# First block of a two-block mixer on one core: gate columns of branches 0 and 2 placed ahead of their branches' paths

## The reference, cut to what matters

```python
h = _rmsnorm(x, mix_norm[l])
proj = (h @ w_in[l])                       # 2820 branch columns, then 3 * 1024 gate columns
ret_c, fox_c, rwkv_c, gate_c = split(proj)
y_ret  = retention branch(ret_c)           # 256 wide
y_fox  = forgetting attention(fox_c)       # 256 wide
y_rwkv = recurrent branch(rwkv_c)          # 256 wide
gates = sigmoid(gate_c)                    # (512, 3, 1024)
merged = gates[:, 0] * (y_ret @ p_ret[l]) + gates[:, 1] * (y_fox @ p_fox[l]) + gates[:, 2] * (y_rwkv @ p_rwkv[l])
x = x + merged @ w_out[l]
... feed-forward on the normed x
```

## Time and profile before

| what | value |
|---|---|
| runs | 3406.28, 3402.62, 3405.69 us |
| span of the profiled execution | 3410.4 us |
| TensorE busy | 3157.1 us (93%) |
| TensorE weight load busy | 2477.1 us (73%) |
| VectorE busy | 1743.8 us (51%) |
| ScalarE busy | 1298.9 us (38%) |

### The profile page before, as it was taken

One profiled execution on the slowest core, in us unless ns is written; L12 is line 12 of the kernel. 1 busy time (PEld: TensorE's weight loads), 2 busy tenths in 40 slices (PEclk: granted clock), 3 DMA queues, 4 the chain that ended last, 5 costly groups with the idle time before them and its releaser, 6 DMA issues.

```text
span 3410.4 us, 37439 instructions
## 1 busy us (share of the span) xinstructions
PE 3157.1 (93%) x14958; PEld 2477.1 (73%) x14958; DVE 1743.8 (51%) x2453; ACT 1298.9 (38%) x2009; POOL 14.9 (0%) x22
## 2 busy tenths in 40 slices
PE   6998999999999988999999999998679799979997
PEld 5566777788886656867888887776368587867886
DVE  4345434555433454425555334446665444548995
ACT  3133323433231332323333224445343533346883
POOL 0000000000000000000000000000000000000000
PEclk9898989999999989979999999999889899999998
DMA  4111102222332111002222321111100001248991
GB/s 154 43 34 50 38 22 68 93 99 96 95 102 82 44 34 53 26 32 93 97 95 98 117 98 63 56 62 37 37 32 32 31 26 56 100 180 312 388 360 56
DMA packets 77629, 306.13 MB, mean 90 GB/s; under 512 B 8208, under 2 KB 13072, under 8 KB 65680
## 3 DMA queue, kind: packets, MB, share of 16 engines
q1 hardware_dynamic: 69056, 284.88, 23.5%
q10 hardware_dynamic: 5808, 9.41, 0.8%
q0 software_dynamic: 2592, 9.44, 0.8%
HBM read 295.83 MB, written 7.86 MB: 89 GB/s over the span
## 4 chain that ended last, share of the span: by engine, by line
PE 82%; DVE 8%; ACT 5%; issue 4%; DMA 1%; ACTq 0%; POOL 0%; POOLq 0%; DVEq 0%
PE bank L371 19%; PE bank L372 18%; PE bank L373 18%; PE bank L366 2%; PE bank L368 2%; PE bank L367 2%; ACT flow_head L390 2%; DVE flow_rest L401 1%; PE bank L1140 1%; PE bank L2363 1%; PE bank L1831 1%; PE bank L1153 1%; PE bank L1913 1%; PE bank L2376 1%; PE bank L1047 1%
## 5 line engine op out<-in xcount | busy, mean ns | idle before, releaser
L371 PE MATMUL bank<-h_head,flow_head 128*128 128x512 f32 x2144 | 913.7, 426 | 26.9 <-DVE flow_rest L401 24.6
L401 DVE TENSOR_TENSOR flow_rest<-flow_raw,flow_head 128x1024 fp32r<-128x1024 f32 (+2 forms) x372 | 438.6, 1179 | 976.8 <-ACT flow_head L390 976.7
L372 PE MATMUL bank<-h_rest,flow_head 128*128 128x512 f32 x2144 | 853.5, 398 | 0.0
L373 PE MATMUL bank<-h_head,flow_rest 128*128 128x512 f32 x2144 | 853.1, 398 | 0.0
L390 ACT ACTIVATE flow_head<-flow_raw 128x1024 fp32r<-128x1024 f32 (+2 forms) x372 | 379.3, 1020 | 704.0 <-PE bank L373 701.5
L371 PEld LDWEIGHTS bank<-h_head,flow_head 128*128 128x128 f32 x2144 | 413.9, 193 | 154.9 <-issue 70.4
L372 PEld LDWEIGHTS bank<-h_rest,flow_head 128*128 128x128 f32 x2144 | 414.1, 193 | 89.7 <-issue 16.6
L373 PEld LDWEIGHTS bank<-h_head,flow_rest 128*128 128x128 f32 x2144 | 412.8, 193 | 91.0
L371 PE MATMUL bank<-ff_head,flow_head 128*128 128x512 f32 x352 | 136.9, 389 | 0.0
L372 PE MATMUL bank<-ff_rest,flow_head 128*128 128x512 f32 x352 | 136.9, 389 | 0.0
L373 PE MATMUL bank<-ff_head,flow_rest 128*128 128x512 f32 x352 | 136.9, 389 | 0.0
(11 more groups left out here) (601 smaller groups left out, 4805.7 us busy)
## 6 DMA issues: line engine op xcount, KB each, us to landing
flow_raw<-in_w_in SPq DMA_DIRECT2D x176, 512.0 KB, 3.2
ring<-in_experts SPq DMA_DIRECT2D x84, 1024.0 KB, 7.2
flow_raw<-in_w_gate_up SPq DMA_DIRECT2D x88, 512.0 KB, 3.2
flow_raw<-in_w_down SPq DMA_DIRECT2D x32, 512.0 KB, 3.4
flow_raw<-in_w_out SPq DMA_DIRECT2D x24, 512.0 KB, 3.2
flow_raw<-in_paths SPq DMA_DIRECT2D x24, 256.0 KB, 2.6
flow_raw<-in_w_down SPq DMA_DIRECT2D x16, 384.0 KB, 3.0
flow_raw<-in_path_b SPq DMA_DIRECT2D x8, 512.0 KB, 3.2
```

The costliest lines, as they stand in the source:

```text
L371: nc.tensor.matmul(ps[u.bank][:, :], wh[:, c:c + P], head, start=start, stop=False)
L372: nc.tensor.matmul(ps[u.bank][:, :], wh[:, c:c + P], rest, start=False, stop=False)
L373: last = nc.tensor.matmul(ps[u.bank][:, :], wr[:, c:c + P], head, start=False, stop=stop)
L401: nc.vector.tensor_tensor(self.parts_of[p.slot][1][:, 0:p.words], p.raw, f32(self.parts_of[p.slot][0][:, 0:p.words]), ALU.subtract).then_i ...
```

## The change

In a layer the order becomes: 22 projection units; 8 gate units of branch 0 (ticks 176 to 240); 8 path units of branch 0 (240 to 256); branch 1 as before (256 to 336); 8 gate units of branch 2 (336 to 400); 8 path units of branch 2 (400 to 416). Banks 6 and 7 serve all of these. Gates of branch 0 stay in `acc`, those of branch 2 in two new places and `sgf`; one of the new places lies over `lora`, so the second layer loads its part of `lora` again behind `table_a`, and retention waits for both. The stretches become: retention ticks 66 to 130, attention 130 to 242, recurrent branch 242 to 400 (the end that paces it is now that of branch 2's gate units).

```diff
-        pe.wait_ge(*k.table_a.at(16 * (l + 1)))
+        pe.wait_ge(*k.table_a.at(16 + 32 * l))
...
+    k.gate_early, k.gate_late = at("gate_early", 67, (4, S)), at("gate_late", 18, (2, S))
...
+            a.dma_start(k.lora[:, l, :], dram["lora_1"][:, l, :]).then_inc(*k.table_a.up(16))
...
-    k.times[l] = [flow.units[k.units_of[l][c]].end for c in (FOX_UNIT - 1, RWKV_UNIT - 1, GATE_UNIT - 1)]
+    for i in range(DC):
+        last = gate_unit(k, l, 0, i, dram)
+    k.times[l] = [flow.units[m].end for m in (k.units_of[l][FOX_UNIT + 7], last)]
+    k.times[l].insert(0, flow.units[k.units_of[l][FOX_UNIT - 1]].end)
+
+def gate_of(k, b, i):
+    if b == 0:
+        return k.acc[:, i, :]
+    if b == 1:
+        return k.sgf[:, i % 2, :]
+    return k.gate_early[:, i, :] if i < 4 else k.gate_late[:, i - 4, :] if i < 6 else k.sgf[:, i - 6, :]
+
+def gate_unit(k, l, b, i, dram):
+    nc, flow = k.nc, k.flow
+    piece, dst = flow.piece(dram["w_in"][l, GATE_UNIT + b * DC + i]), gate_of(k, b, i)
+    def scale(v, m):
+        return nc.vector.tensor_tensor(dst, k.ps[flow.units[m].bank][:, :], k.root[:, :], ALU.mult)
+    def squash(a, m):
+        k.tables(EXP_TANH)
+        a.wait_ge(*flow.emptied_by(m))
+        nc.scalar.activation(dst, dst, ACT.Tanh, scale=0.5).then_inc(*k.squashed.up())
+    return flow.unit(6 + i % 2, [(piece, c * P) for c in range(DC)], normed(k, 2 * l)(False), [(1, scale)], [(2, squash)])
+
 def branch_units(k, l, b, dram):
+    if b == 2:
+        for i in range(DC):
+            k.gates_end = gate_unit(k, l, b, i, dram)
     for i0 in range(0, DC, 2):
-        pieces = [flow.piece(dram["w_in"][l, GATE_UNIT + b * DC + i]) for i in (i0, i0 + 1)]
+        if b == 1:
+            gate_unit(k, l, b, i0, dram)
+            gate_unit(k, l, b, i0 + 1, dram)
         both = flow.piece(dram["paths"][l, b, i0 // 2])
-        gates = []
-        for q in range(2):
-            ...  (scale and squash into sgf)
-            gates.append(flow.unit((6 if b < 2 else 4) + q, ...))
...
-        end = flow.units[paths_end[l][1]].end
+        end = flow.units[paths_end[l][3]].end
```

More of the change, by code:

```diff
@@ L579, in vector_part @@
         flow.dve(rot(0))
-        v.wait_ge(*k.table_a.at(16 * (l + 1)))
+        v.wait_ge(*k.table_a.at(16 + 32 * l))
         for j in range(4):
@@ L1449, in mixer_units @@
         k.units_of[l][0:FOX_UNIT], k.units_of[l][FOX_UNIT:RWKV_UNIT], k.units_of[l][RWKV_UNIT:GATE_UNIT])
-    k.times[l] = [flow.units[k.units_of[l][c]].end for c in (FOX_UNIT - 1, RWKV_UNIT - 1, GATE_UNIT - 1)]
+    for i in range(DC):
[18 more added lines that the diff above has]
+    return flow.unit(6 + i % 2, [(piece, c * P) for c in range(DC)], normed(k, 2 * l)(False), [(1, scale)], [(2, squash)])
 def branch_units(k, l, b, dram):
     nc, flow, v, a = k.nc, k.flow, k.v, k.a
-    operand = normed(k, 2 * l)
+    if b == 2:
+        for i in range(DC):
+            k.gates_end = gate_unit(k, l, b, i, dram)
     for i0 in range(0, DC, 2):
-        pieces = [flow.piece(dram["w_in"][l, GATE_UNIT + b * DC + i]) for i in (i0, i0 + 1)]
+        if b == 1:
+            gate_unit(k, l, b, i0, dram)
+            gate_unit(k, l, b, i0 + 1, dram)
         both = flow.piece(dram["paths"][l, b, i0 // 2])
-        gates = []
-        for q in range(2):
[L1463 to L1472, removed]
         for q in range(2):
@@ L1481, in gated @@
                 v.wait_ge(*k.squashed.at((l * 3 + b) * DC + i + 1))
-                dst = k.acc[:, i, :] if b == 0 else k.sgf[:, q, :]
-                return nc.vector.scalar_tensor_tensor(dst, k.sgf[:, q, :], 1.0, k.ps[flow.units[m].bank][:, :], ALU.add, ALU.mult)
+                gate = gate_of(k, b, i)
+                return nc.vector.scalar_tensor_tensor(gate, gate, 1.0, k.ps[flow.units[m].bank][:, :], ALU.add, ALU.mult)
             def add(v, m, q=q, i=i):
                 v.wait_ge(*flow.emptied_by(m))
-                nc.vector.tensor_tensor(k.acc[:, i, :], k.acc[:, i, :], k.sgf[:, q, :], ALU.add).then_inc(*k.added.up())
+                nc.vector.tensor_tensor(k.acc[:, i, :], k.acc[:, i, :], gate_of(k, b, i), ALU.add).then_inc(*k.added.up())
             def heads(a, m, i=i):
@@ L2640, in third_memory @@
     k.ple = [at(f"ple_{n}", c, (4, S)) for n, c in enumerate((56, 60))]
-    k.router_landed, k.stored = k.loaded.over(80), [k.table_a.over(32), k.table_2.over(64)]
+    k.router_landed, k.stored = k.loaded.over(80), [k.table_a.over(48), k.table_2.over(64)]
     k.picked_landed = [Mark(sems, f"picked_landed_{n}") for n in range(2)]
@@ L3244, in stream @@
         mixer_units(k, l, dram)
-        paths_end.append([branch_units(k, l, b, dram) for b in range(3)])
+        paths_end.append([branch_units(k, l, b, dram) for b in range(3)] + [k.gates_end])
         def merged(first, l=l):
```

## The result

The changed kernel takes 3429.7 us (median of 5 runs, 3421.5 to 3442.0) against 3405.7 us of the kernel before, measured beside it: ratio 1.0069, 95% interval 1.0049 to 1.0088. A second comparison gave 1.0054 (1.0039 to 1.0069). It is slower, as the forecast's likeliest case said, but by 18 to 24 us where 7 were forecast. That is outside the forecast's own 3409 to 3421 us and nearest to rival C (3434).

The account below looks back on a forecast made before the run. TensorE bounds the kernel, 82% of the chain that ended last. Per layer 14.0 us won and 17.5 us lost make 3.5 us slower, 7 in all: 3413 us, own range 3409 to 3421, overall range 3384 to 3436.

Parts of the forecast that it names:

- rival C: Costs in full: inputs lose 13 us, end 10, only 9 won; 14 us per layer slower, 3434 us; chance 0.14.
- The end of the branch (+7.5): Behind the recurrent branch's result, VectorE and ScalarE in turns over eight path units: 7.5 us lost per layer, ends 4.5 and 11.
- The inputs (+10): Recurrent branch's inputs: branch 0's path units wait for banks VectorE evicts only between blocks; 10 us lost per layer, ends 3 and 14.
- The attention loop (-8.6): Attention loop: more stream ticks shorten gaps and half-clock stretches; 8.6 us won per layer, ends 3 and 13.
- The 1.5 us for waits hidden by modelled ends: Attention loop: shorter waits that the modelled ends hide may give 1.5 us.
- Retention (-4.0): Retention with 64 ticks for 48: 2.3 - 2.7 + 3.4 + 1, 4.0 us won per layer, ends 0 and 13.
- the loop's waits (2.7 worse): Retention's loop: five bursts in place of three, gaps 7.1 against 4.4 us, 2.7 us worse.
- the 2.3 us wait on line 586 goes: Retention's rotation: 12.8 ticks beside it in place of 9.6, 2.2 us more, so the 2.3 us wait goes.
- The 3.4 us of clock: Retention: the first half-clock stretch starts at the gap expected to go, so 3.4 us won.
- The hidden 1 us: Retention: 1 us won from hidden waits.
- Pairs, inverse and scan (-1.0): These stages keep their ticks; gate units alone there bring fewer evictions, 1 us won, ends 3 lost and 3 won.
- Rival A, cover pays: Denser stream keeps full clock in both loops and waits go: 11 us won per layer, 3384 us; chance 0.28 with neighbouring outcomes.

Follow-up runs that it names:

- the kernel with all three mends: Changed kernel with later split points in retention, two more eviction points in the inputs, branch 2's heads and rests due 3 and 5 ticks after: 3373.0 us, ratio 0.9892.
- the middle course: Against the kernel before: four gate units of branch 0 ahead, branch 2's split four and four around the recurrent end, later heads and rests: 3408.9 us, ratio 1.0015.

## Why the prediction was right in direction and short in size

The end of the branch (+7.5) was right: its chain of turns gave 31.5 us from the complete result to the end of w_out's eighth tick, and the trace has 622.7 - 591.65 = 31.0. Mending the turns took the loss away. By the stage marks of the table it is 5.5 and 6.3.

The inputs (+10) came as told: for gated one wait of 3.4 us and one of 8.1 ("one near 8 us"), and line 990 at 338.48, 48.9 us later than before where the branch starts 37.6 later, so 11.3 us late (11.8 forecast). Behind it more was given back than forecast: from line 1004 to the pairs the stretch is 5.0 us shorter. 7.2 us in place of 10.

The attention loop (-8.6) was right in mechanism: no wait on line 758, one short stretch at half clock. The 1.5 us for waits hidden by modelled ends did not show: 6.9 and 7.0.

Retention (-4.0) is the step that failed, with a loss of 1.8 and 4.4 us in its place: 5.8 and 8.4 us a layer, where the forecast of the layers' sum is short by 9.1 and 6.7. Of its four parts the loop's waits (2.7 worse) were near: 7.7 against 4.4 us. That "the 2.3 us wait on line 586 goes" was wrong: it stayed at 2.2 us. I had laid the old order of VectorE over the longer stretch, but the points where it takes up splits are fractions of the stretch, so with 64 ticks a due split moved ahead of the third column, and VectorE stood 3.8 us for its head. The 3.4 us of clock came from the claim that this gap would go; it did not, and with 10 us of waits in retention its loop's mean clock was 0.89 and 0.87 (0.85 and 0.88 before). The hidden 1 us did not show. Later runs show how far the two go together: the clock of retention is 1.00 in all four traces in which no wait is left, and 0.85 to 0.94 in its loop with 7 to 10 us of waits.

Pairs, inverse and scan (-1.0) came out at +4.8 and -0.9. Pairs and inverse lost 1.7 and 2.0 us, which no experiment took apart; the scan's part is the clock's.

The rest is not a stage: the two layers' 22.8 us less 8.4 us in the start, the join and the second block (1817.2 us in before's trace, 1811.3 in after's, by the same program) give the traces' 14.4, and before's trace lies 7 us above its median. I had subtracted a constant from the span for that; the half clock of one execution can't be carried over. There was luck in it too: inputs and end were priced too high by 2.8 and by 1.2 to 2.0 us a layer, which hid part of what retention, pairs and scan cost. Rival C's 3434 is near by luck alone, for it put the loss into inputs (13) and end (10), and retention made it.

Rival A, cover pays, failed in retention, where cover doesn't shorten a wait made by order. The Trainium skill's rule (TensorE: Matmul & The Clock Gate, HAM oscillation), that idling between bursts lowers the clock and a dense stream keeps it, held for retention, 1.00 without gaps, and again not for the scan: in the kernel with all three mends its mean clock was 0.82 in one layer and 0.71 in the other, without a gap.
```profile
491.30:547.80 56.50, 56.38 (x317) 0.82 0.05 15
1452.20:1516.10 63.90, 63.77 (x317) 0.71 0.04 13
```

## What to carry to other kernels

Before work is moved to cover a wait, ask whether the wait ends with work or with order: here two moved hooks (points where VectorE takes up due stream work), which let it do the operation of the critical chain before it stands for a split, were worth 25 to 27 us in the kernel before and 31 to 36 in the changed one, while the moved units gained 7 us a layer in one loop and lost them where eight short units with evictions stood side by side. Short units need the engines behind them to take their evictions at once; two more points for it, or a later due time for the second half of the chain, took the loss away. And where hooks are fractions of a stretch, every change of its length reorders them: lay the new fractions out before pricing it.

## What the runs showed of the hardware

A gap costs more than itself: taking 10.0 us of waits out of retention shortened it by 16.1 and 17.1 us, since the granted clock no longer fell to half. A stretch without gaps isn't safe either: the same scan, 316 or 317 matmuls that wait for nothing, took 56.5, 57.9 and 63.9 us in different layers and traces of the changed order, with a mean clock of 0.82, 0.79 and 0.71, and 60.7 or 60.8 us (0.75) in all five traces with the old order up to the scan. Executions of one kernel range over 20 us (3398 to 3419 for the middle course), most of what such a change is worth, and one trace is one draw of it.
